# Dilated attention of a two-model transformer kernel: transposes moved behind a projection, and the output projection begun during its last period

## What is computed

```python
def dilated_attention(h, w_in, w_o, rel_bias):
    proj = (h @ w_in).reshape(B, S, N_GROUPS, 3, DIL_HEADS, DIL_HEAD_DIM)   # 3 groups, q k v, 16 heads of 64
    for g, (window, dilation) in enumerate(((128, 1), (512, 4), (2048, 16))):
        # logits = q k^T / 8 + bias inside the dilated window; lse = logsumexp(logits)
        # o = softmax(logits) v
        ...
    alpha = softmax(stack(lses), axis=0)              # weight of each group, per token and head
    o = sum(alpha[..., None] * stack(outs), axis=0)
    return o.reshape(B, S, DIL_WIDTH) @ w_o
```

## Time and profile before

| | us |
|---|---|
| median of 3 runs | 3871.89 |
| lowest, highest | 3866.84, 3872.97 |
| the profiled execution | 3879.0 |
| its span, first to last instruction | 3876.9 |
| PE busy | 3619.1 (93%) |
| DVE busy | 2017.1 (52%) |
| ACT busy | 1333.8 (34%) |

### The profile page before, as it was taken

The page is one execution under the profiler, slowest core; times in us unless marked ns, Lnnn a source line. Parts: engine busy times, 40 slices in busy tenths (PEclk is TensorE's granted clock), DMA queues, the critical chain, the costliest instruction groups (busy, mean ns, idle before and its releaser), DMA issues.

```text
span 3876.9 us, 40995 instructions
## 1 busy us (share of the span) xinstructions
PE 3619.1 (93%) x16372; PEld 2876.8 (74%) x16372; DVE 2017.1 (52%) x3608; ACT 1333.8 (34%) x2291; POOL 128.0 (3%) x126
## 2 busy tenths in 40 slices
PE   5899999899999999988999999999999889869998
PEld 4647888666888788866678887888777777757886
DVE  7856756676766654466763236324633222345234
ACT  3563323343423332334442233223322232233222
POOL 2330000000000000001100000000000000000000
PEclk9999999989999999999999999999999999979999
DMA  6214554413555455320022222222222222122221
GB/s 244 98 44 160 203 191 180 151 56 110 195 185 195 174 195 195 114 74 33 22 66 99 99 95 80 99 94 97 86 73 63 78 63 62 45 63 87 98 93 65
DMA packets 155466, 429.06 MB, mean 111 GB/s; under 512 B 45467, under 2 KB 50523, under 8 KB 155276
## 3 DMA queue, kind: packets, MB, share of 16 engines
q1 hardware_dynamic: 155276, 426.45, 31.5%
HBM read 423.98 MB, written 2.40 MB: 110 GB/s over the span
## 4 chain that ended last, share of the span: by engine, by line
PE 81%; DVE 11%; ACT 4%; DMA 2%; issue 1%; SPq 1%; POOL 0%; ACTq 0%; DVEq 0%; POOLq 0%
PE ps L412 23%; PE ps L414 23%; PE ps L413 23%; ACT SD L1306 1%; PE ps L786 1%; PE ps L711 1%; DMA lse<-small 1%; DMA small<-lse 1%; PE ps L456 1%; PE ps L449 1%; DVE TT L1483 1%; DVE HL L1468 1%; DVE wlo L1416 1%; PE ps L751 1%; DVE X L1569 1%
## 5 line engine op out<-in xcount | busy, mean ns | idle before, releaser
L412 PE MATMUL ps<-HH,whi 128*128 128x512 f32 x3168 | 1264.9, 399 | 58.9 <-DVE HL L1468 28.1
L413 PE MATMUL ps<-HL,whi 128*128 128x512 f32 x3168 | 1245.9, 393 | 0.0
L414 PE MATMUL ps<-HH,wlo 128*128 128x512 f32 x3168 | 1245.5, 393 | 0.0
L1416 DVE TENSOR_TENSOR wlo<-wraw,whi 128x1024 fp32r<-128x1024 f32 x526 | 643.8, 1224 | 702.5 <-ACT whi L891 702.3
L891 ACT ACTIVATE whi<-wraw 128x1024 fp32r<-128x1024 f32 x548 | 576.1, 1053 | 652.7 <-PE ps L414 640.3
L412 PEld LDWEIGHTS ps<-HH,whi 128*128 128x128 f32 x3168 | 603.0, 190 | 216.7 <-issue 63.3
L414 PEld LDWEIGHTS ps<-HH,wlo 128*128 128x128 f32 x3168 | 602.5, 190 | 128.8
L413 PEld LDWEIGHTS ps<-HL,whi 128*128 128x128 f32 x3168 | 603.4, 190 | 127.2 <-issue 4.6
L1404 DVE CUSTOM_DVE_ANT_0 mraw<-mraw,CB 128x1024 f32<-128x1024 f32 x224 | 282.6, 1263 | 0.6 <-DMA mraw<-mst 0.6
L1602 DVE TENSOR_TENSOR TT<-TT,ps 128x512 f32<-128x512 f32 x116 | 79.7, 687 | 217.1 <-PE ps L414 187.8
L412 PE MATMUL ps<-PHf,whi 128*128 128x512 f32 x352 | 136.9, 389 | 0.0
(11 more groups left out here) (325 smaller groups left out, 3931.3 us busy)
## 6 DMA issues: line engine op xcount, KB each, us to landing
wraw<-wst SPq DMA_DIRECT2D x548, 512.0 KB, 3.4
mraw<-mst SPq DMA_DIRECT2D x224, 512.0 KB, 3.4
MR<-mst SPq DMA_DIRECT2D x16, 512.0 KB, 13.6
X<-xt SPq DMA_DIRECT2D x8, 256.0 KB, 5.1
BB<-bvec SPq DMA_DIRECT2D x8, 256.0 KB, 3.7
TT<-lse SPq DMA_DIRECT2D x16, 128.0 KB, 3.0
out<-X SPq DMA_DIRECT2D x8, 256.0 KB, 2.0
CB<-crow SPq DMA_DIRECT2D x2, 512.0 KB, 4.5
```

Source lines behind the costliest of these rows:

```text
L412: e.matmul(o[key], wh, sh(k), start=k == 0, stop=False)
L413: e.matmul(o[key], wh, sl(k), start=False, stop=False)
L414: ins = e.matmul(o[key], wl, sh(k), start=False, stop=k == nk - 1)
L1416: e.tensor_tensor(wlo[:, x % SPLIT, :], wraw[:, x % RAW, :], whi[:, x % SPLIT, :].bitcast(F32), ALU.subtract).then_inc(*wlo_made.up(x))
```

## The change

It has four parts. First, the transposes of a value tile (`turn_values`) and the copy to VN (`values_in`) stand one projection later, for the last of the three in step 0 of the next period. Second, the transposes of the probabilities (`turn_probs`) are taken out of `values` and stand one projection ahead of it: those of head 0 in step 6, those of head 1 in step 7, the products in steps 7 and 8. RB follows, in DVE's steps 7 and 8, and so do the inversion (step 1 of the next period) and `finish` (step 3). Third, `column_of` stands inside projection 5, behind its second k. Fourth, the output projection is cut: three output tiles run over k 0 to 5 in step 5 of the last period and over k 6 in step 7, four more over k 0 to 6 behind the last value products; then all seven over k 7, then the eighth tile. The weight stream has the same tiles in that order. The splits of HH and HL move to step 2 of the last period.

```diff
@@ dil_groups
-    return gs + [(8, [("dil_o", i)]) for i in range(8)]
+    gs += [(range(7), [("dil_o", i) for i in ms]) for ms in ((0, 1, 2), (3, 4, 5, 6))]
+    return gs + [(range(7, 8), [("dil_o", i) for i in range(7)]), (8, [("dil_o", 7)])]
@@ tensor_engine: proj
-                for k in range(nk):
+                for k in ks or range(nk):
...
-                        if k == 0:
-                            o[key] = take(key, main[0])
+                        o[key] = take(key, main[0]) if k == 0 else ps[:, bank_of[key], :]
@@ tensor_engine: dilated
-                    elif step == 4:
-                        column_of(c)
                     elif step == 6:
+                        turn_probs(c, 0)
+                    elif step == 7:
                         take(("od", c), ob)
                         values(c, 0)
-                    elif step == 7:
+                        turn_probs(c, 1)
+                        row_of(("sr", c), cs[:, 0, :, :], a_mix, ("ex", c, 1))
+                    elif step == 8:
                         values(c, 1)
-                        row_of(("sr", c), cs[:, 0, :, :], a_mix, ("ex", c, 1))
...
+                def out_part(ms, ks):
+                    proj([("o", "dil", m) for m in ms], 8, hh, hl, lambda k: (v_mix, ("dy", k)), None, ks)
+
                 for c in range(8):
                     for step in range(9):
                         if c < 7:
-                            head_proj(c + 1, step)
+                            head_proj(c + 1, step, (lambda k: column_of(c) if k == 1 else None) if step == 5 else None)
+                            if step in (3, 6):
+                                turn_values(c + 1, step // 3 - 1)
+                        elif step == 5:
+                            out_part(range(3), range(6))
+                            column_of(c)
+                        elif step == 7:
+                            out_part(range(3), range(6, 7))
+                        if step == 0:
+                            turn_values(c, 2)
                         attend(c, step)
+                main[0] = pool_b
+                out_part(range(3, 7), range(7))
+                out_part(range(7), range(7, 8))
+                main[0] = ob
+                out_part((7,), range(8))
@@ scalar_engine: out_proj, dilated
-                    feed(8)
+                    if stage != "dil" or m in (0, 4):
+                        feed(8)
...
-                        elif 2 <= step:
-                            keep(step - 2)
+                        elif step == 2:
+                            for m in range(6):
+                                keep(m)
+                                if m in (3, 5):
+                                    feed(8)
+                        elif step == 4:
+                            feed(8)
+                        elif step == 6:
+                            keep(6)
...
+                feed(24)
                 keep(7)
@@ vector_engine: dilated
                         if c < 7:
                             head_proj(c + 1, step)
-                        elif step >= 2:
-                            keep(step - 2)
+                            if step in (3, 6):
+                                values_in(c + 1, step // 3 - 1)
+                        elif step == 6:
+                            keep(6)
+                        if step == 0:
+                            values_in(c, 2)
                         if step < 2:
                             biased(c, step)
                         elif step == 2:
                             row_out(("mr", c), 0, max_out)
+                            if c == 7:
+                                for m in range(6):
+                                    keep(m)
+                                    if m in (3, 5):
+                                        feed(8)
                         elif step == 3:
                             top(c)
-                        elif step == 4:
+                        elif step == 5:
                             column_in(c)
-                        elif step == 6:
+                        elif step == 7:
                             spread_probs(c, 0)
-                        elif step == 7:
-                            spread_probs(c, 1)
                             row_out(("sr", c), 2, sum_out)
                         elif step == 8:
-                            invert(c)
+                            spread_probs(c, 1)
                         if step == 1 and c:
+                            invert(c - 1)
+                        elif step == 3 and c:
                             finish(c - 1)
+                        elif step == 4 and c == 7:
+                            feed(8)
+                feed(16)
+                invert(7)
+                feed(8)
                 finish(7)
                 keep(7)
@@ sync_engine: dilated
-                        if c < 7:
+                        if c < 7 or n < 4:
                             feed(8)
```

More of the change, by code:

```diff
@@ L81, in tile_list @@
 def tile_list():
-    return [(name, k, m) for nk, cols in plan() for k in range(nk) for name, m in cols]
+    return [(name, k, m) for nk, cols in plan() for k in (nk if isinstance(nk, range) else range(nk)) for name, m in cols]
 def columns():
@@ L402, in weights, with proj @@
                 return whi[:, b % SPLIT, sl], wlo[:, b % SPLIT, sl], [("w", b)] if last else []
-            def proj(keys, nk, sh, sl, ready, between=None):
+            def proj(keys, nk, sh, sl, ready, between=None, ks=None):
                 o = {}
-                for k in range(nk):
+                for k in ks or range(nk):
                     for key in keys:
                         wh, wl, names = weights(1)
-                        if k == 0:
-                            o[key] = take(key, main[0])
+                        o[key] = take(key, main[0]) if k == 0 else ps[:, bank_of[key], :]
                         lane.wait_ge(*ready(k))
@@ L730, in dilated, with head_proj, turn_values @@
                 proj([("dl", 0, n) for n in range(4)], 8, hh, hl, ready)
-                def head_proj(c, n):
+                def head_proj(c, n, between=None):
                     if c or n >= 4:
[L734 to L741, removed]
+                        proj([("dl", c, n)], 8, hh, hl, ready, between)
+                def turn_values(c, g):
+                    o = take(("vt", c, g), main[0])
+                    lane.wait_ge(a_mix, ("vt", c, g))
+                    for j in range(4):
+                        ins = e.transpose(o[:, 128 * j:128 * j + 128], VT[:, g, 128 * j:128 * j + 128], C["ident"][:])
+                    ins.then_inc(*mm_done.up(("vt", c, g)))
                 def logits(c, hh_):
@@ L768, in logits, with turn_probs @@
                     ins.then_inc(*mm_done.up(("lg", c, hh_, 3)))
-                def values(c, hh_):
-                    vn, sd = VN[c % 2], SD[hh_]
+                def turn_probs(c, hh_):
+                    sd = SD[hh_]
                     for z3 in range(3):
@@ L778, in values @@
                         ins.then_inc(*mm_done.up(("pt", c, hh_, z3)))
+                def values(c, hh_):
+                    vn = VN[c % 2]
                     oh_ = ps[64 * hh_:64 * hh_ + 64, bank_of[("od", c)], :]
@@ L830, in dilated @@
                     head_proj(0, n)
+                    if n in (3, 6):
+                        turn_values(0, n // 3 - 1)
+                def out_part(ms, ks):
+                    proj([("o", "dil", m) for m in ms], 8, hh, hl, lambda k: (v_mix, ("dy", k)), None, ks)
                 for c in range(8):
@@ L863, in tensor_engine @@
             dilated()
-            out_proj("dil", hh, hl, lambda k: (v_mix, ("dy", k)))
             post_norm(1, 1)
@@ L1971, in head_proj, with values_in @@
                         freed[key] = ((v_mix, ("dk", c, g)),)
[L1972 to L1979, removed]
+                def values_in(c, g):
+                    key = ("vt", c, g)
+                    lane.wait_ge(mm_done, key)
+                    if c >= 2:
+                        lane.wait_ge(mm_done, ("od", c - 2, 1))
+                    e.tensor_copy(VN[c % 2][:, 4 * g:4 * g + 4, :], bank(key).rearrange("p (j f) -> p j f", j=4)).then_inc(
+                        *v_mix.up(("vn", c, g)))
+                    freed[key] = ((v_mix, ("vn", c, g)),)
                 def biased(c, hh_):
@@ L2055, in dilated @@
                     head_proj(0, n)
+                    if n in (3, 6):
+                        values_in(0, n // 3 - 1)
                 for c in range(8):
@@ L2370, in sync_engine @@
             dilated()
-            feed(64 + 528)
+            feed(32 + 528)
             for m in range(8):
```

1 line of the change is left out of this document (added).

## The result

| | before | after |
|---|---|---|
| median, us | 3871.36 (3866.84 to 3872.97, 4 runs) | 3806.81 (3799.49 to 3808.53, 4 runs) |
| ratio | | 0.9831, 95% interval 0.9814 to 0.9849 |
| the profiled execution, and its span | 3879.0, 3876.9 | 3806.5, 3804.4 |
| PE busy | 3619.1 (93%) | 3600.5 (95%) |
| whole period 1 | 81 us | 74.0 us |

The forecast was 3802 with a range of 3780 to 3838. The spans differ by 72.5 us. Another 55.0 lie between that point and the last VT group (3379.3 before, 3316.85 after), and 9.9 from there to the FFN's first product. The changed code so gave 64.9 in this pair of profiles; the medians differ by 64.6.

What follows compares the result with a forecast made beforehand. The prediction took the matrix engine PE as the bound, busy 72.68 of 81 us per period, so its waits are paid in full. Terms summed to 69.7 off 3879.0, giving 3809, less 7.1 a median of 3802; range 3780 to 3838.

Steps and rivals of the forecast that it cites:

- VT transposes, +17.2: Dilated stage, VT transposes behind the next projection: all 23 PE waits for the VT copy go, 17.2 us gained.
- Probability transposes, +31.2 and +15.4: Periods 0 to 6, transposes one projection earlier: seven PD waits go, 31.2 us, and the slow clock behind them, 15.4.
- RB, -9.5: First head's last four value products: PE waits 1.35 us for RB, made later by DVE, seven times, 9.5 us lost.
- Slow clock behind RB, -5.6: Small products after the RB wait: half of a 1.6 us slowing in each period, 5.6 us lost in all.
- Column, +9, and slow clock behind it, +2: Column inside projection 5: seven waits shrink from 10.9 to some 2 us, gaining 9; less slow clock behind gains 2.
- inverses and finishing one step later: SP's inverses in step 2 of the next period, three weight loads right after them, before the maxima: costed at nothing.
- rival B: Three loads after the inverses delay the maxima's transfers, answer up to 4.6 us late: 3825 us with half, 3847 at most; chance 0.14.
- The tail, +10: Last period and output projection: norm's first number at t 92.5 instead of 104.8; gain 12, of which 10 us taken.
- A: Rival: RB comes in time, no slow clock follows, and the tail gives 13: 3784 us; chance 0.12.
- C: Rival: the tail gains nothing, eaten by DVE's sums and small transfers: 3812 us; chance 0.66 together with the forecast.
- D: Rival: PE at half clock from the RB wait into the next period's first two projections: 3886 us; chance 0.04.
- E: Rival: ACT's in-order queue holds PD back past projection 7 too, so PD waits stay: 3834 us; chance 0.04.

Runs made afterwards that it cites:

- The late inverses: Changed kernel with SP's inverses issued behind the tops instead of ahead of the maxima in periods 1 to 6, finish in DVE's step 6: 3792.05 us, ratio to before 0.9801.

## Why the prediction was right, step by step

The time was 4.8 us above the forecast, and the terms that carry it stand. One step failed, and another failed the other way. That the two nearly cancel is luck: 13.1 us too much at the column stand against 7.6 too little elsewhere.

- *VT transposes, +17.2:* right, 23 waits gone, and worth more than the idle time listed for them: the 24 groups take 18.22 us from start to start instead of 38.57, 20.35 less. Alone the part gave 25.8, with less column wait and less slow clock behind it.
- *Probability transposes, +31.2 and +15.4:* right. Summed over periods 0 to 6 of the kernel before, the first head's value products exceed the second's 3.42 us by 15.4; none of that is left after. The run with them put back lost 40.6: 46.6 less 10.7 for RB is 35.9, the last period's wait and slow value products are 5.5, and its column waits are 0.9 shorter.
- *RB, -9.5:* right, 1.32 seven times for a predicted 1.35, and from the named cause: RB stands behind wlo and the QK copy, and with RB ahead of them the wait is gone. From start to start the delay is 1.53, 10.7 in seven, with the next term in it.
- *Slow clock behind RB, -5.6:* failed, it is 0.35 in all. Of the two rows it was taken from, the 1.62 wait without slowing was like what came, but at the column waits of the same size were followed by the half clock four times of six. By the Trainium skill ("TensorE: Matmul & The Clock Gate", PE-mode transpose) transposes do not count as activity in the same way. As the prediction reads it, this stretch would have been slow each time; the trace disagrees, with 8 small products and 12 transposes (1.46 us) at full pace directly behind the wait.
- *Column, +9, and slow clock behind it, +2:* this step failed. Measured are -0.1 and -2.0. That PE comes later is right; that the answer takes no longer than before is not. What was wrong is "I cost it at nothing", said of inverses and finishing one step later: three loads get ahead of the maxima and hold them 2.65 us. It is rival B's mechanism at a smaller size than its 4.6, in the six periods named. The late inverses show it: without the collision no column wait is left in periods 0 to 5, and the time falls by 14.8 us.
- *The tail, +10:* 9.9 in the profiles; taken out by itself it is worth 11.2 in the same stretch. The clocking held in the main: column at t 29.3 (forecast 27.9), last value products at t 48.9 (49.5), the seven features' sums behind PE, a wait of 9.0 at the norm. Part of that is two errors that cancel: the first value products begin at t 40.3 instead of 38.6, but run at full clock, 3.42 us instead of the 6.1 taken.

These measured terms, 20.35 + 31.2 + 15.4 - 10.7 - 0.1 - 2.0 + 9.9, sum to 64.0 of the 64.9 that the changed code gave; 0.9 is left over. The sum of 69.7 was 4.8 above the 64.9: 13.1 us too much at the column and 0.1 at the tail, 4.4 too little at RB and its clock, 3.15 too little at VT, and the 0.9. The span also got 7.4 us ahead of the stage, which no term names; the 7.1 taken for the profiled execution of before lying above its median is about that.

Of A the half without a slow clock came, RB in time did not. C, D and E did not come: the tail gave its 10 us, none of the periods 0 to 6 fell to the half clock for longer than one projection, and PD was in time. In the last period the half clock does last longer, from 3321.7 to 3335.2, through waits of 0.73, 0.72 and 1.06 us among small products and into the output projection.

## What to carry to other kernels

When transposes or other hand-overs are moved a stage ahead of their users, follow each moved step through every queue in which it stands, the transfer queue above all: a small latency-bound transfer behind three bulk loads cost here what the change was to win at the column, and an answer that waits for a slow producer blocks what is queued behind it (YF behind RB). Place releases of a shared bank ahead of work that waits. Once the waits are gone, read the busy share of a whole period: 69.18 of 69.18 us says that it is time to look elsewhere.

## What the runs showed that was not expected

Three queued loads of 512 KB add 2.65 us to a dependent pair of small transfers, and four in place of one add 3.74 to a single one, though one load takes 3.4 us from issue to landing in the median. Loads are not the only thing that can hold them: in period 3 of the kernel before the same way took 5.77 us instead of 3.7, with the DMA engines busy only 0.07 of it, and that is the column wait of 3.21 us in the earlier trace rows. What held it was not found. And equal waits need not cost the same: a wait of 1.58 us inside a projection cost 1.6 us more by half clock behind it, one of 1.59 nothing, and seven of 1.32 amid small products next to nothing. Why the one and not the other, no run here tells.
